# New tables for the order of the expert work in a two-layer decoder step, without the zero matmuls on TensorE

## What is computed

```python
q = (xt @ w_q).reshape(PEER_BLOCK, PEER_HEADS, 2, PEER_HALF)      # 8 heads
s1 = jnp.einsum('thk,nk->thn', q[:, :, 0], sub_keys[0])           # 128 keys each
s2 = jnp.einsum('thk,nk->thn', q[:, :, 1], sub_keys[1])
t1, i1 = lax.top_k(s1, 16); t2, i2 = lax.top_k(s2, 16)
cand = t1[..., :, None] + t2[..., None, :]
top, ci = lax.top_k(cand, 16)                                     # 16 of 256 pairs
idx = i1[ci // 16] * 128 + i2[ci % 16]                            # one of 16384 experts
g = jax.nn.softmax(top)
act = gelu(einsum('thkd,td->thk', u_tab[idx], xt))
out = einsum('thk,thkd->td', g * act, v_tab[idx])
```

## Time and profile before

| | us |
|---|---|
| median of 3 runs | 2014.44 (2013.32 to 2024.56) |
| span of the profiled execution | 2136.8 |
| PE busy | 1549.0 (72%) |
| DVE busy | 1321.9 (62%) |
| POOL busy | 1185.7 (55%) |
| ACT busy | 353.4 (17%) |

### The profile page before, as it was taken

How to read it: one execution, slowest core, us unless ns; L and a number is a source line. 1 busy time by engine, 2 the same in 40 slices (tenths; PEclk the granted TensorE clock), 3 DMA queues, 4 the chain that set the end, 5 groups by cost and what they waited for, 6 DMA issues and landing times.

```text
span 2136.8 us, 25746 instructions
## 1 busy us (share of the span) xinstructions
PE 1549.0 (72%) x9280; PEld 752.4 (35%) x9280; DVE 1321.9 (62%) x3189; ACT 353.4 (17%) x934; POOL 1185.7 (55%) x1097
## 2 busy tenths in 40 slices
...
GB/s 371 314 236 346 365 330 347 391 396 382 347 346 348 359 404 373 361 414 347 382 212 345 271 375 401 378 345 349 367 337 303 352 309 343 402 417 370 377 349 306
DMA packets 213941, 751.57 MB, mean 352 GB/s; under 512 B 27236, under 2 KB 35628, under 8 KB 213816
## 3 DMA queue, kind: packets, MB, share of 16 engines
q0 software_dynamic: 155136, 564.20, 69.8%
...
...
HBM read 747.74 MB, written 2.10 MB: 351 GB/s over the span
## 4 chain that ended last, share of the span: by engine, by line
PE 43%; DVE 14%; DMA 13%; issue 12%; POOL 8%; another core or an unknown queue 7%; ACT 2%; SPq 1%; DVEq 0%; POOLq 0%; ACTq 0%
PE yacc L1274 13%; DMA vring<-in_peer_v,expert 6%; POOL uring L813 4%; PE pp L1062 4%; DVE uring L2046 4%; POOL vring L813 3%; PE pp L1036 3%; PE pp L1125 3%; PE pq L1125 2%; PE ps L1160 2%; PE ps L870 2%; PE pp L1197 1%; DMA uring<-in_peer_u,expert 1%; PE ps L1184 1%
## 5 line engine op out<-in xcount | busy, mean ns | idle before, releaser
L813 POOL DMA_INDIRECT uring<-in_peer_u,expert x512 | 571.5, 1116 | 471.1 <-DVE dots L2046 191.1
L1274 PE MATMUL yacc<-vring,diag 64*64 64x512 f32 x4096 | 659.3, 727 | 230.1 <-DMA vring<-in_peer_v,expert 118.0
L813 POOL DMA_INDIRECT vring<-in_peer_v,expert x512 | 542.2, 1059 | 430.6 <-PE yacc L1274 263.3
L2046 DVE CUSTOM_DVE_ANT_0 uring<-uring,h 128x1024 f32<-128x1024 f32 x512 | 614.9, 1226 | 201.2 <-DMA uring<-in_peer_u,expert 175.7
L1274 PEld LDWEIGHTS yacc<-vring,diag 64*64 64x64 f32 x4096 | 158.0, 154 | 589.1 <-issue 345.5
L1566 ACT ACTIVATE diag<-cst,wts 128x64 f32<-128x64 f32 (+1 forms) x528 | 155.4, 338 | 470.4 <-PE yacc L1274 229.9
L1062 PE MATMUL pp<-hT,wring 128*128 128x128 f32 x1024 | 128.9, 287 | 10.4 <-DMA wring<-in_peer_w_q 4.6
L1062 PEld LDWEIGHTS pp<-hT,wring 128*128 128x128 f32 x1024 | 124.1, 202 | 28.1 <-issue 26.2
L1929 DVE TENSOR_REDUCE arena<-arena 128x16 f32<-128x1024 f32 x64 | 77.8, 1216 | 63.8 <-ACT arena L1505 58.8
L1317 ACT ACTIVATE arena<-ps 128x512 f32<-128x512 f32 (+6 forms) x77 | 39.9, 532 | 253.4 <-remote 76.9
L1125 PE MATMUL pp<-w_uk,arena 128*128 128x512 f32 x128 | 75.3, 677 | 3.4 <-issue 2.7
...
## 6 DMA issues: line engine op xcount, KB each, us to landing
...
uring<-in_peer_u,expert POOLq DMA_INDIRECT x512
vring<-in_peer_v,expert POOLq DMA_INDIRECT x512
```

The lines of the kernel that those rows point to most:

```text
L813: pool.indirect_dma_start(ring[:, slot % RING, :], None, table[n // 3], bass.IndirectOffsetOnAxis(ap=idx, axis=0)).then_inc(land[slot % RI ...
L1274: last = pe.matmul(yacc[64 * q:64 * q + 64, r], diag[at, slot % RING, :], v[at, 512 * q:512 * q + 512], start=first, stop=final)
L2046: dve.tensor_tensor_reduce(u, u, rows_h[:, :], 1.0, 0.0, ALU.mult, ALU.add, dots[:, p % 2, i:i + 1]).then_inc(u_used, 1)
```

## The change

All five tables are replaced. In the new ones no spot has an N, so `keep_clock` is never called and its 82 matmuls are gone. One line is new: `load_mod_bias` first waits until POOL's five memsets at its start are through. Lines of the new kernel are 24 or 25 lower. Everything else is the same: the units, their number, the rings, the gathers and chunks.

```diff
 PLAN_PE = """
-52:N 75:N 120:N 148:N 152:N 157:V 158:V 159:V 160:V 169:VV 170:VV 171:V 173:V 174:V 176:V 180:V 184:V 189:VV 192:VVV
...
+181:VVVVVVVVVVVVVVVV 192:VVVVVVVVV 199:VV 200:VVVVV 209:VV 210:VV 224:VVV 229:VV 231:VV 252:VV 272:VVV 282:VV
...
             def load_mod_bias(row):
 
                 _, l, j = MODS[MOD_ROW * row]
+                sp.wait_ge(cleared, 5)
```

More of the change, by code:

```diff
@@ new lines @@
+353:VVVVVVV 355:VV 356:VVV 361:VVV 371:VV 374:VV 375:V 389:VVVVV 397:VV 409:VVVV 414:VVV 418:VV 420:VV 436:V 440:V
+444:V 448:V 452:VVV 480:VV 490:V 495:VV 500:VV 518:V 521:VVV 526:VV 528:V 549:VV 557:VVV 559:V 561:V 572:VVVVVVVVVVVVV
+573:V 583:V 584:V 588:VVVVVVVVVV 590:VV 591:VV 596:VV 621:VV 623:VV 631:VVVVV 632:VV 642:V 646:VVVVVVVVVV 648:VV
+649:VV 654:VV 668:VVVVVVVVVVV 678:V 682:V 683:VVVVVVVVVVV 685:VV 686:V 691:VV 695:VVVV 699:VV 701:VVVVVV 708:V 725:V
+766:VV 771:V 776:VVV 781:VVV 799:V 802:VVV 807:VVV 830:VV 832:VV 845:VVVVVVVVVVVVVVVVV 847:V 853:VV 854:V 860:V
@@ new lines @@
+424:D 425:D 426:T 429:DDDDDDDDDDDD 431:DD 432:DD 445:TDDDDDDD 454:DD 455:DD 465:D 469:DDDTDDDDDDDDD 471:DD 472:DDDD
+477:DD 493:T 495:DDDDD 496:DD 499:D 503:D 504:DDDDDDDTDDDDDD 506:YDDD 510:DD 514:DDDD 516:D 540:TDDDDDDDDDD 554:DDD
+557:DDD 561:TDD 571:DDDDD 579:DD 581:DDDDD 586:D 590:DTDDDDDD 597:DDDDD 598:D 600:D 606:DD 607:D 613:TD 614:DDDDDDD
+616:DD 617:DDD 625:DDD 640:TDDDDDDD 650:DD 654:DDDDDDTDDDDDD 656:DD 657:DDDDD 662:DDDD 684:TDDDDDDDDD 685:DDD 688:DD
+689:DDY 697:TDDDDDDDDDDDDD 705:D 709:DD 724:TDDDDDDD 727:DDDDDDDDDTDDDDDDDD 749:TDDDDDDD 756:DD 760:DDD 762:DD 766:DD
@@ L151 @@
+771:T 776:DDDDDDDDDDDDD 786:D 790:D 793:D 804:TDDDDDDDDD
+805:DDDDDDDTDDDDDDDDDDDDDDDDTDDDDDDDDDDDDDDDDTDDDDDDDDDDDDDTDDDDDDDDDYDD
 """
 PLAN_DVE = """
[L153 to L155 removed]
@@ L176 @@
-2196:U 2199:U 2203:UUUPWUUUUUUUUPW
+199:U 271:UUUUUUU 314:U 319:U 323:U 326:U 332:U 334:U 344:U 349:U 350:P 351:WU 352:U 355:U 358:U 361:U 373:U
+420:UUUUUU 442:UUUUUPWUU 460:U 466:UUU 470:UU 474:UU 477:UU 478:U 485:UUPUWUU 486:UUU 490:UUUUUUU 495:U 509:U
+513:UUPUWUUUUU 573:U 595:U 636:U 639:UUU 681:U 682:UU 683:P 684:W 703:U 713:U 714:U 715:U 745:UU 762:U 765:U 771:U
+782:U 785:UUUUUUPUW 807:UUUUUUU 845:UU 847:UU 852:UUUUPUWUU 863:UUUUU 864:U 865:U 868:UU 870:U 871:U 890:UUUP 892:W
+893:U 895:U 903:UUU 907:UU 923:U 925:U 926:U 945:U 948:U 950:U 951:UUUPUWUU 954:UUUUU 970:U 972:U 986:UU 990:UUUPWUUUU
@@ new lines @@
+1011:UU 1028:UUUUU 1056:UUUUUPWUU 1077:U 1081:UUUUUUUU 1112:U 1115:U 1121:U 1123:U 1145:U 1147:P 1148:W 1163:U 1168:UU
+1169:UU 1179:U 1193:U 1195:UUUUUU 1200:UUU 1202:PUW 1203:U 1205:U 1206:U 1210:U 1211:U 1212:U 1222:UU 1268:UUUU
+1290:UU 1291:U 1292:P 1293:W 1299:UU 1307:UUUUUU 1309:U 1311:U 1312:U 1314:UU 1315:U 1317:U 1319:U 1320:PUWUU 1334:U
+1337:U 1347:U 1422:U 1426:U 1433:U 1435:U 1441:UUUUUU 1442:PUW 1443:UU 1445:UUU 1446:UU 1448:U 1449:UUU 1451:U 1452:U
+1468:UUP 1470:W 1477:UUU 1495:U 1499:UUUUUUUU 1520:UU 1523:U 1537:UUPUWUUUUUU 1557:U 1565:UUUUUUUPW 1590:UUUUUUU
@@ new lines @@
+1624:UU 1625:U 1626:U 1627:U 1630:U 1660:UU 1661:U 1662:PUWUU 1694:U 1696:UUUUUU 1700:UU 1701:UUU 1703:U 1704:P
+1706:WUU 1723:U 1726:U 1728:U 1736:UU 1769:UUUUUU 1795:U 1801:U 1804:U 1805:PUW 1808:UUU 1810:U 1812:U 1813:U 1815:UUU
+1816:UUU 1819:U 1820:U 1821:U 1822:PUW 1829:U 1835:U 1868:U 1910:U 1936:U 1942:UUUUUU 1943:U 1944:UUUUPUWUUU 1946:UUU
+1947:U 1952:U 1964:U 1969:UU 1978:UU 1985:UUPUW 1993:UUU 2007:UUUUUUUUU 2047:UUPW 2051:UUUUUUUUPUWUUUUUUU 2058:U
+2072:UUUUUUUPWUUUUUUUUUU 2111:U 2115:UU 2133:UUUUP 2134:W 2137:UUUU 2161:UUUUUUUUUUU 2175:P 2176:W
```

97 lines of the change are left out of this document (23 added, 74 removed).

## The result

The median of 19 runs is 2032.25 us for the changed kernel (2019.23 to 2044.56) and 2013.06 us for the kernel before (1999.02 to 2029.62). The ratio is 1.0087, with a 95% interval of 1.0065 to 1.0109. The forecast was 2012, no change, with a range from 1945 to 2080; the time lies in that range, but the kernel became slower where no change was forecast.

The account below looks back on a forecast made before the run. The prediction took transfers to bound most stretches, DVE k19–34, and neither the first cache and two woven stretches. Its terms summed to −2 us, 2134.8 of 2136.8 profiled; times 0.943 gave 2013, stated as 2012, range 1945 to 2080.

Parts of the forecast that it names:

- The tail: k149 to the last picks, taken as near transfer-limited: −91 us; then the end, with more gathers waiting: +90 us.
- rival two: k149 to the last picks is held by its own steps, losing 55 us instead of 91: 2059 us, chance 0.23.
- the prediction's −8: The end: POOL, which stood 8.6 us before the sample's first gathers, has other gathers to issue meanwhile: −8 us.
- k40–56: 27 gathers fewer, 36 us by transfers alone; 13 dots off DVE's path, 16 us: −16 taken, bounds 0 and −36.
- The wait on the memsets: Loads of the bias rows: waiting for five memsets costs nothing; if wrong, the first stretch grows by up to 10 us.
- The +15 of k107–128: k107–128: 11 gathers more at a DMA share of 0.98, with no room: +15 us.
- the terms from k90 to k148: k90–97 −8, k98–106 +4, k107–128 +15, k129–132 0, k133–141 +3, k142–148 +6 us.
- the room: Transfer time below 390 GB/s that takes extra gathers free: 52 us in k98–106, 34.7 in k133–141, 15.1 in k142–148.
- rival one: First cache and two woven stretches: longer runs of units fill half the unused room, 54 us off: 1962 us, chance 0.27.
- the count of gathers by the end of a stretch: Every stretch: gathers each order lets out by its end, differences priced at 1.34 us each where transfers limit.
- its sign of being wrong: k90–97 or k129–132, which lose most of their gathers, grow; they were forecast at −8 and 0 us.
- The third rival: Without zero matmuls the clock falls in k133–141, k67–89 and k107–128, +33 us: 2044 us, chance 0.08.

Follow-up runs that it names:

- The mixed kernel: Kernel before with its tables kept up to k148 and all five tables of the changed kernel from k149 on: 0.9905 to before, median 1998 us.
- the disturbed profile: First profile of the unchanged kernel before, the one the prediction was based on: one execution of 2136.8 us.
- the second one: The unchanged kernel before, run once more for a profile: span 2008.5 us.
- the edits on after: Changed kernel with dots put ahead of the mixes, 1.0090, sums moved too, 1.0093; dots put ahead of the picks, 1.0162, POOL's list changed too, 1.0138.

## Why the prediction was wrong, by its own steps

**What held.** The tail: k149 to the last picks lost 105 us (91 forecast), the end gained 88.6 (90 forecast), for 70 gathers fewer and 73 more. So transfers bound that stretch, at 1.5 us a gather, and rival two, that its own steps hold it, is refuted: 162.7 us, where over 204 was its mark. The mixed kernel shows the gain of the tail by itself, 0.9905. The end had idle transfers to give, as the prediction's −8 says: its share was 0.86 at 325 GB/s and is 0.99 at 390 now. k40–56 moved as forecast and by more (−26.2 against −16): 25 gathers fewer for 26.2 us, between the 16 by dots and the 34 by transfers. The wait on the memsets costs nothing that shows: with before's tables k0–18 takes 151.2 to 159.5 us in five profiles with it and 151.9 to 158.0 in seven without.

The +15 of k107–128 came near for a reason that is only half of it, and that is luck. The prediction priced gathers there. The 8 that came pay for 10.7 of the 18.9 us, but 8 sums more (694 records instead of 630) also keep PE busy 13.0 us longer, in a stretch where it was busy for 126.93 of 129.1 us; no run separates the two.

**What failed: the terms from k90 to k148, +20 forecast and +77 measured.** Three steps of the working are at fault.

The first is the room, length × (1 − rate / 390): "265.1 × (1 − 314/390) = 52 us" and 34.7 us in the woven stretches, 15.1 in k142–148. It was read from the disturbed profile. In the second one the woven stretches carry 368 and 391 GB/s at shares of 0.98 and 1.00: there is next to no room, and rival one falls with it. In the woven two that cost the forecast little, as the 49 gathers that were to take the room didn't come (146 → 148 and 153 → 148). It shows in k142–148: +6 was forecast, and 14 gathers more cost 15.7 us, 1.12 each. That stretch has a share of 0.96 at 351 GB/s, so a rate under 390 isn't yet room. The sign was there in rows 1: 7% of the chain had an unknown releaser, and the span was 6% over the median. The prediction scaled that away by 0.943, as if the loss lay evenly.

The second is the count of gathers by the end of a stretch. The prediction took 21 and 26 gathers out of k90–97 and k129–132 because the new table puts their sums at the start of the next step. But PE reaches those sums while DVE is still at the picks: in k90–97 14 of the stretch's 21 sums run behind PE's last matmul of its own steps. In the trace k90–97 issues 36 gathers, not 13, and k129–132 39, not 4. The end of a step on one engine isn't the end on another.

The third is the one that the runs show best, and it has the largest misses, +11.1 against −8 in k90–97 and +13.6 against 0 in k129–132. The prediction named this as its sign of being wrong ("then a head's dots or a wait that I don't see holds them"), and both are there. "DVE's own steps fill 45.63 of 65.1 us, so at most −20" counts dots per stretch. What matters is whether a dot stands where DVE waits anyway or inside a chain for which the others wait. In before nine dots moved from the one place to the other, with the same count per stretch, cost 12.3 us there and 0.7% of the kernel; in after, 11 and 12 dots stand in such places. The same mistake in small hides in other stretches: sums and dots in longer runs, with places between them in which an engine takes up no unit, so that rings of 7 run full and POOL stands still. Before with its dots put behind the mixes, which makes such a place, loses 1.04%. In k133–141, with the largest part of the 40 us, POOL's waits for a place that a dot frees, before and after, are

```profile
POOL uring L813 <- DVE dots L2046: 0.9, 1, 0.9
```

```profile
POOL uring L789 <- DVE dots L2022: 13.6, 7, 4.1
```

and no run was made on that stretch.

How much of the loss each of these is in the changed kernel was not settled by undoing them: the edits on after left or moved a hole (1.0090 and 1.0093) or made it worse (1.0162, 1.0138). In each, some unit stayed where the next engine had to wait for it. That both kinds of place cost time is shown on before. In the changed kernel the stretches from the scores to the last picks are longer by 12.4 and 13.2 us, of which 2.7 and 9.4 us would also be the price of the 2 and 7 gathers more; the rest, in k98–106 and k133–141 above all, is argued only, from the shares and waits.

**The third rival**, a lower clock, stayed short of its marks: 0.85 in k133–141 and 0.87 in k67–89, where under 0.84 and under 0.80 were the signs. Before without the zero matmuls has 0.86 in k133–141, a fall of 0.03, and no kernel without them was measurably slower for it. The Trainium skill ("TensorE: Matmul & The Clock Gate", section "HAM oscillation — how this bites in real kernels") says that waits for DMA between bursts of matmuls send the array back to half its speed; the trace agrees in direction, with 0.89 to 0.86. By that rule taking the fillers out should have cost time; the runs of before without them, 0.9935 and 0.9963, say the opposite.
